# Where the norm sums of a two-block model stand, and in which order its stages open

## What is computed

```python
# first stack, 2 layers
h = rmsnorm(x, norm_g); proj = h @ w_in          # 7592 columns
log_cum = cumsum(log_sigmoid(a_f + b_f))         # a_f: 8 "forget" columns
y_a, y_b, y_c = three attentions of 8 heads (the first one with log_cum)
merged = sum_n sigmoid(gate_n) * ((y_n * silu(z_n)) @ w_branch[n])
x = x + merged @ w_out
x = rmsnorm(x, final_g)                          # between the stacks
# second stack, 2 layers
h = rmsnorm(x, mix_norm_g); u = h @ w_in_2
retention (with rotary q, k), state space, gated linear attention, mLSTM
x = x + merged @ w_out_2
h = rmsnorm(x, ffn_norm_g)
layer 0: x = x + (silu(h @ w1) * (h @ w3)) @ w2  # 2816 hidden
layer 1: x = x + top-2 of 8 experts of that form
x = rmsnorm(x, final_norm_g)
```

## Time and profile before

| | us |
|---|---|
| three timed runs | 2573.23, 2573.83 (median), 2574.51 |
| the profiled execution | 2568.81 |
| its span | 2567.0 |
| PE busy with matmuls | 2390.4 |
| DVE busy | 1699.7 |
| ACT busy | 1263.9 |
| granted clock, mean share of full | 0.965 |

### The profile page before, as it was taken

How to read it: one execution, slowest core, us unless ns; L and a number is a source line. 1 busy time by engine, 2 the same in 40 slices (tenths; PEclk the granted TensorE clock), 3 DMA queues, 4 the chain that set the end, 5 groups by cost and what they waited for, 6 DMA issues and landing times.

```text
span 2567.0 us, 38254 instructions
## 1 busy us (share of the span) xinstructions
PE 2390.4 (93%) x15110; PEld 2016.9 (79%) x15110; DVE 1699.7 (66%) x2630; ACT 1263.9 (49%) x1793; POOL 18.1 (1%) x35
## 2 busy tenths in 40 slices
PE   8999989999999989779998989789999999999997
PEld 7878888878788978679997878677777777777775
DVE  4455674456676557663325557658889889898896
ACT  4435534535543333342214343337767667677664
POOL 0000000000000000000000000000000000000000
PEclk9999999999999989889998989889999999999999
DMA  5433333433373433254443433219989999898893
GB/s 174 128 115 99 99 115 124 136 115 116 102 173 116 149 99 99 99 181 136 160 141 114 145 110 101 99 36 412 353 331 354 344 341 349 339 352 345 332 352 136
DMA packets 255352, 489.12 MB, mean 191 GB/s; under 512 B 35096, under 2 KB 208696, under 8 KB 221128
## 3 DMA queue, kind: packets, MB, share of 16 engines
q1 hardware_dynamic: 249648, 483.87, 53.5%
q10 hardware_dynamic: 4872, 1.09, 0.2%
q0 software_dynamic: 656, 1.71, 0.2%
HBM read 485.57 MB, written 1.05 MB: 190 GB/s over the span
## 4 chain that ended last, share of the span: by engine, by line
PE 70%; DVE 10%; ACT 3%; issue 2%; DMA 1%; DVEq 0%; SPq 0%; ACTq 0%
PE bank L1024 24%; PE bank L689 19%; PE bank L714 9%; PE bank L559 5%; DVE memr L1838 3%; PE bank L541 3%; PE bank L977 2%; PE bank L728 1%; PE bank L497 1%; PE bank L664 1%; PE bank L1065 1%; DVE mem_high L2313 1%; DVE mem_high L2271 1%; PE bank L474 1%; ACT memr L1453 1%
## 5 line engine op out<-in xcount | busy, mean ns | idle before, releaser
L1024 PE MATMUL bank<-memr 128*128 128x256 f32 (+5 forms) x8016 | 1060.5, 293 | 78.4 <-DVE memr L1838 29.3
L1024 PEld LDWEIGHTS bank<-memr 128*128 128x128 f32 (+3 forms) x8016 | 1006.2, 191 | 124.9 <-DVE memr L1838 34.4
L883 DVE TENSOR_TENSOR memr_tail<-mem_tail,memr_ring 128x2048 fp32r<-128x2048 f32 x198 | 451.9, 2288 | 60.8 <-ACT memr_ring L780 58.6
L689 PE MATMUL bank<-memr_ring,memr 128*104 128x512 f32 x1492 | 467.3, 399 | 3.2 <-DVE memr L888 3.2
L1838 DVE TENSOR_TENSOR memr<-mem_low,memr 128x1024 fp32r<-128x1024 f32 (+2 forms) x316 | 378.9, 1215 | 131.3 <-ACT memr L1453 131.0
L780 ACT CAST memr_ring<-mem_tail 128x2048 fp32r<-128x2048 f32 x198 | 379.4, 1916 | 130.9 <-PE bank L689 88.9
L1453 ACT CAST memr<-mem_low 128x1024 fp32r<-128x1024 f32 (+2 forms) x316 | 324.5, 1042 | 186.0 <-PE bank L1024 173.4
L689 PEld LDWEIGHTS bank<-memr_ring,memr 128*104 128x104 f32 x1492 | 250.7, 168 | 95.2 <-issue 3.3
L714 PE MATMUL bank<-memr_ring,memr 128*104 128x512 f32 x752 | 242.4, 400 | 1.7 <-DVE memr_ring L883 1.7
L689 PE MATMUL bank<-memr_tail,memr 128*104 128x512 f32 x536 | 211.4, 394 | 0.0
L714 PEld LDWEIGHTS bank<-memr_ring,memr 128*104 128x104 f32 x752 | 125.3, 168 | 43.3 <-DVE memr_ring L883 1.9
(11 more groups left out here) (247 smaller groups left out, 2221.6 us busy)
## 6 DMA issues: line engine op xcount, KB each, us to landing
mem_tail<-in_moe SPq DMA_DIRECT2D x198, 1024.0 KB, 4.9
mem_low<-in_w_in SPq DMA_DIRECT2D x112, 1024.0 KB, 5.0
mem_high<-in_moe SPq DMA_DIRECT2D x33, 1024.0 KB, 4.8
mem_low<-in_moe SPq DMA_DIRECT2D x33, 1024.0 KB, 4.9
mem_high<-in_ffn_w SPq DMA_DIRECT2D x30, 1024.0 KB, 8.3
mem_low<-in_w_branch SPq DMA_DIRECT2D x20, 1024.0 KB, 4.9
mem_low<-in_w_out SPq DMA_DIRECT2D x16, 1024.0 KB, 5.2
mem_low<-in_w_in SPq DMA_DIRECT2D x6, 512.0 KB, 3.8
```

Source lines behind the costliest of these rows:

```text
L689: ins = pe.matmul(ACC[g % 2][0:CAP, :], h_[e % 2][:, kk, :], w_[:, 512 * k:512 * k + 512], start=(kk == 0 and i == 0), stop=(kk == KT - 1 ...
L883: TTn(raw_r[n % RAW], raw[n % RAW], hi_f[n % HI], ALU.subtract).then_inc(family("m_split"), 1)
L1024: ins = pe.matmul(out(bank), lhsT, rhs, start=((k, i) == order[0]), stop=((k, i) == order[-1]))
```

## The change

1. **Norm sums.** `square_sum` adds the square of tile j-1 right after unit j of `wo` or `wo2`; the last one stands behind the last unit. The sum is built in bank `XB` (between the stacks a second one in `OB`) and `root_of_sum` reads it there. The first norm of all uses the same form without anything between; the norm ahead of the second mixing layer and the last norm stay as they were.
2. **Opening.** `gemm3_two` issues the first two units of a stage side by side: all products with `hh` of unit 0, then of unit 1, then those with `hl` of unit 0 and of unit 1. It is used for `fq` (both layers) and `rq` (both layers). Feed-forward tile 0 gets the same order for its halves. DVE now scales all tiles first and makes the low parts after.
3. **Forget columns.** `ff` and `z 0` come right after `fq`; the chain on DVE and ACT is cut in pieces that lie between the `fk` units.
4. **First feed-forward tile.** Its high parts are cast after the squares 6 and 7 of the residual (ACT), its low parts made ahead of the norm (DVE), and each half has a semaphore of its own.
5. **Rotary.** The matmul for `rk 1` stands after unit `gz 0`.

```diff
+            def gemm3_two(names, ch, cols, m, lo, n, key):
...
+                two = [open_group(name) for name in names]
+                kinds = ((high, hh, "h_high"), (low, hh, None), (high, hl, "h_ready"))
+                for part in ((0, 1), (2,)):
+                    for name, bank, c0 in zip(names, two, cols):
+                        for k in range(KT):
+                            for i in part:
+                                w_, h_, event = kinds[i]
+                                if event and name is names[0]:
+                                    pe.wait_ge(*at(event, key, k))
+                                ins = pe.matmul(bank[0:m, lo:n], w_[:, k, c0:c0 + m], h_[:, k, lo:n], ...
+            def square_sum(bank, key, k, n, lo=0, weights=None):
+                pe.wait_ge(*at("squares", key, k))
+                ins = pe.matmul(bank[:, lo:n], weights(k) if weights else const("ones"), sq[:, k, lo:n], ...
+            def mix_sum(k):
+                square_sum(XB, ("mix", 0), k, T, 0, lambda k: pc("final_w", k).broadcast_to((P, P)))
+                square_sum(OB, ("mix", 0), k, T)
...
+                    if nm == "fq":
+                        ch = split_chunk(win, l, 1536, 1672)
+                        feat3(("ff", l), ch, 0, 8, TA)
+                        feat3(("z", l, 0), ch, 8, P, TA, lo=m0)
...
+                    if l == DEPTH - 1:
+                        if j == 0:
+                            pe.wait_ge(*at("final_w"))
+                        else:
+                            mix_sum(j - 1)
+                    elif j:
+                        square_sum(XB, l + 1, j - 1, TA)
...
+                gemm3_two((("rq", l, 0), ("rq", l, 1)), ch, (0, P), P, 0, T, ("mix", l))
...
                     feat3(("gz", l, j), ch, j % 2 * P, P, T)
+                    if j == 0:
+                        rope2(("rk", l, 1))
...
                     feat3(("wo2", l, j), ch, j % 2 * P, P, T, key=None if j else ("merged2", l))
+                    if j:
+                        square_sum(XB, ("ffn", l), j - 1, T)
+                square_sum(XB, ("ffn", l), KT - 1, T)
... ACT
+                def first_up(k):
+                    if k >= KT - 2:
+                        up_high(0, k - (KT - 2))
... DVE, in both norms
-                    if then and k:
-                        then(k - 1)
                 if then:
-                    then(KT - 1)
+                    for k in range(KT):
+                        then(k)
... DVE, after the last wo2
+                    if l == 0 and j == KT - 1:
+                        low_up(0, 0)
+                        low_up(0, 1)
```

More of the change, by code:

```diff
@@ L1510, in _ @@
                         ahead(nm, l, j)
+                        if nm == "fk" and j == 1:
+                            st.settle()
+                            st(A(asc[0:8, 2, :], asc[0:8, 1, :], ACT.Ln, bias=1.0), sig("logf_ln", l))
+                    if nm == "fq":
+                        act.wait_ge(*evacuated("ff", l))
+                        st(A(asc[0:8, 0, :], tsc[0:8, 3, :], ACT.Abs))
+                        z_tile(0)
+                        st.settle()
+                        st(A(asc[0:8, 1, :], asc[0:8, 0, :], ACT.Exp, scale=-1.0))
                 for c in range(2):
@@ L1515, in _ @@
                     ahead("fv", l, 2, c)
-                act.wait_ge(*evacuated("ff", l))
-                st(A(asc[0:8, 0, :], tsc[0:8, 0, :], ACT.Abs))
-                st.settle()
-                st(A(asc[0:8, 1, :], asc[0:8, 0, :], ACT.Exp, scale=-1.0))
-                st.settle()
-                st(A(asc[0:8, 2, :], asc[0:8, 1, :], ACT.Ln, bias=1.0), sig("logf_ln", l))
-                def z_tile(j):
-                    b = full(act, "z", l, j)
-                    st(A(zs[:, j, m0:], b[:, m0:TA], ACT.Tanh, scale=0.5), sig("z_tanh", l, j))
-                    ahead("z", l, j)
-                for j in range(4):
+                for j in range(1, 4):
                     z_tile(j)
@@ L1799, in _, with normalise @@
             st(V.tensor_scalar(fw, fw, EPS, None, ALU.add), sig("final_w"))
-            def normalise(name, slot, gcol, src, dst, tiles, done, n=TA, d0=0, lo=0, then=None):
-                dve.wait_ge(*evacuated(*name))
+            def normalise(root, slot, gcol, src, dst, tiles, done, n=TA, d0=0, lo=0, then=None):
+                dve.wait_ge(*root)
                 st.settle()
@@ L1810, in normalise @@
                        done(i) if done else None)
-                    if then and i:
-                        then(i - 1)
                 if then:
-                    then(KT - 1)
+                    for k in tiles:
+                        then(k)
             def low_tile(key, k, src, slot, n, lo=0):
```

192 lines of the change are left out of this document (115 added, 77 removed).

## The result

| | before | after |
|---|---|---|
| median of four timed runs, us | 2573.53 | 2546.86 |
| the profiled execution | 2568.81 | 2546.35 |
| its span | 2567.0 | 2544.5 |
| PE busy | 2390.4 | 2378.4 |
| span less PE busy | 176.6 | 166.1 |

What follows compares the result with a forecast made beforehand. PE was taken as the bound, busy 2390.4 of 2567.0 us. Terms 14.2 - 2.9 - 5.6 - 2.4 + 2.7 + 1.0 + 1.8 + 2.2 gave 11.0 us won, so 2573.83 became 2562.8; range 2554 to 2571.5.

Steps and rivals of the forecast that it cites:

- The openings: First two units of a stage: 3.0 us won over three, less 0.3, plus 1.0 between the stacks.
- Rival (c): Openings: the clock stays up as PE gets work twice as fast, 13.6 us more won, 2549.2; chance 0.06.
- The first feed-forward tile: Feed-forward tile 0: from last product to tile 0's end 20.5 us instead of 22.3, so 1.8 won.
- 4 or 5: Sign of a right forecast: the feed-forward wait goes down from 10.98 us to 4 or 5.
- The price of a lone matmul: Norm sums between products: each moves the next unit by 0.72 us, where one in a row costs 0.45.
- rival (a): Norm sums: one between two products costs only 0.45 us, so 6.7 more is won, 2556.1; chance 0.08.
- the sign of part 1: Norm sums between products: roots come later, not earlier, by 2.4 to 5.6 us at each seam; a loss.
- The forget columns: Behind ff in both layers: stops of 4.91 and 5.07 us and their low clock vanish, 14.2 won.
- Rival (d): Forget columns: the chain stops PE in its new place too, the 14.2 us is gone, 2577.0; chance 0.06.
- Rotary: Matmul of rk 1 moved behind gz 0: 1.1 us won, twice, so 2.2.
- the only case below 2554: Rival (c), the clock up in the openings, at 2549.2 us; chance 0.06.

Runs made afterwards that it cites:

- a_again: The changed kernel run again with nothing altered, as a yardstick: median 2546.19 us, 0.9904 of the time before.
- o_open: Kernel before, with only part 2 (openings side by side, DVE scaling first) added: 2557.11 us, 0.9950 of the time before.
- o_first: Kernel before, with only part 4 (first feed-forward tile split ahead of the norm) added: 2563.97 us, 0.9976 of the time before.
- u_first: Changed kernel without part 4, the first feed-forward tile split behind the norm again: 2547.45 us, 0.9914 of the time before.
- o_sums: Kernel before, with only part 1 (norm sums between the residual products) added: 2579.77 us, 1.0037 of the time before.
- u_sums: Changed kernel without part 1, all norm sums in a row behind the last product: 2532.44 us, 0.9856 of the time before.
- u_rope: Changed kernel without part 5, both rotary matmuls of rk ahead of gz 0 again: 2543.43 us, 0.9904 of the time before.

## Why the prediction was wrong

**The openings are the step that failed.** The forecast put the gain of an opening at 1.0 us: eight products by 2.9 us after the first scaling, then "6.8 us at 0.23 each" of low clock, then the rest, 11.0 in all. It took what the clock does, and where it does it, as fixed. Ahead of layer 1 the opening took 8.8 us, not 11.0. The low stretch has its old length, but it begins 1.7 us ahead of the first scaling, not 2.9 behind it: of its 6.8 us only 4.04 fall on busy PE, the rest on the reciprocal, the first scaling and the cast, for which PE waits. In the first norm and ahead of the second mixing layer the stretch shrank from 6.8 to 3.4. From the first scaling to the second unit's evacuation the four openings took 11.7, 12.1, 11.3 and 11.9 us and take 9.4, 8.8, 8.9 and 9.5: 10.4 gained, where 3.7 was forecast. In a_again, the same program, they take 10.0, 9.8, 10.1 and 9.7: 7.4 gained, although three of them hold a stretch of 6.8 us. Its opening ahead of layer 1, with the window over the low stretch:

```profile
401.46 3.39 DVE L1889 SCALAR_TENSOR_TENSOR mem_low<-mem_high 128x272 f32<-128x272 f32 x8
411.22 0.37 ACT L1583 COPY mem_high<-bank 64x256 f32<-64x256 f32 x1 [0.17 <-PE bank L1053]
...
401.80:408.60 6.80, 6.04 (x28) 6.07 (x29) 6.80 (x17) 3.31 (x8) 0.00 (x0) 0.50 0.00 0
```

So the price of a product at the low clock was right (28 products in the stretch, where 29 were forecast). What was wrong is that eight would be done ahead of it: it begins with the scalings, and the other 20 run behind it at full speed. The working priced DVE's order and PE's together; alone DVE's brings 12.7, PE's nothing. Rival (c), the clock up in the openings, named the right place, but its condition, 1.00 all through, is not what happened, and openings and first tile together brought 9.3 more than forecast between the profiles, not its 13.6. In o_open, 13.2 us faster, the time that PE stands still is unchanged (177.1 against 176.6), and busy PE is 13.9 shorter; half of what it is less in low stretches (120.2 us instead of 145.7) is 12.8. So nearly all of it is the clock. Why a denser supply in the opening leaves fewer low stretches elsewhere, these runs do not show.

**The first feed-forward tile** was another term off, by the same 11.0: 1.8 forecast. The wait fell by 6.6 to 4.40, as the "4 or 5" named for a right step, and the low stretch there from 10.2 to 3.4. The delays by ACT's cast and DVE's subtraction are as worked out: the root starts 1.98 after the last product (forecast 2.15 to 2.6), the reciprocal, at 1115.06 behind the subtraction, 3.43 (forecast 3.4), and it is done at 5.2, as forecast. From the first scaling to tile 0's end, where the forecast had 11.0, it took 8.7 (9.2 in a_again). From the root to tile 0's end it is 18.7 before and 11.9 after; 12.0 in o_first, and 17.5 in u_first. So the part is worth 5.6 to 6.7 us at its place, alone and in the changed kernel. The timed runs gave 6.4 alone and 1.3 undone: PE's standing still moves by 7.4 and 5.1, but the part raises PE busy, by 2.6 in o_first and by 4.0 between u_first and the changed kernel, and in the second that eats the gain.

**The price of a lone matmul** failed too, and moved the sum by 4.7 us. Forecast 0.72, as "this very situation". It was not: in the earlier trace rows the neighbour waited for a bank, and a sum in `XB` takes no bank from anybody. Periods of the units, by the times at which DVE takes them up: 2.83 us before and 3.26 with a sum between, 3.02 and 3.47 with 272 columns, 3.67 with two sums. So a sum costs 0.43, 0.45 and 0.42. The Trainium skill, "TensorE: Matmul & The Clock Gate", section "Step-by-step: what each phase is for", has the weights of the next matmul loaded during the present one; the trace agrees (0.43 between two products, 0.45 in a row), and the prediction should have asked why a row spoke against it. Its premise for rival (a) held.

Rival (a), a chance of 0.08, wanted 6.7 more from this (6 x 0.27 x 4 is 6.5). 4.7 came at the four seams; the rest went into the first sum of each, whose square is late. So the sign of part 1 stays as forecast. DVE's rows of the last and of the second unit ahead of the experts are 20.03 us apart, before 16.96: 3.07 more, since the first sum, whose square is late, adds 0.9, and five add 0.43. The root comes 1.73 after the last one, before 3.46. Net +1.3; ahead of the feed-forward +1.4, ahead of layer 1 +1.6, between the stacks 5.55 more and 1.24 less, +4.3. Together 8.6, where 13.3 was forecast, and o_sums measured 8.9. So PE is full there: six of the eight sums push the last product out by as much as they take from behind it, and the chain of last evacuation, square and sum, 1.7 us that ran beneath the other sums, now stands alone. In the changed kernel the part costs 13.8; of the 15.0 between the spans 6.7 is standing still, the rest the clock (8.9, see u_sums). Why it falls so is not shown.

**The forget columns** went as worked out: both stops are gone with the low clock behind them. From the second unit of the opening to the root of the low-rank norm behind `z` the two traces draw apart by 7.5 us in layer 0 and 6.6 in layer 1: 14.1 against 14.2, and the same 14.1 in a_again. Alone 18.0, undone 11.5: PE's standing still moves by 9.3 and 10.5, near the 9.98 of the earlier trace rows, PE busy by 6.9 and 2.3. Rival (d), a new stop behind `ff`, did not occur.

**Rotary**: forecast +2.2; at its place the part gained 0.7 and 1.0, 1.7 in all, and 4.5 in a_again, where no low stretch falls on the two places. The timed runs can't show it. Before, PE stands for 2.08 and 1.36 there (3.4 us, the second is the earlier trace rows); now `gz 0` waits 2.08 and `gz 1` 0.67. A low stretch of 3.4 us lies on the place before and after (`gz 0` takes 4.61 us). Rows of the changed kernel at that place:

```profile
785.86 4.61 PE L1028 MATMUL bank<-memr 128*128 128x256 f32 x24 [2.08 <-DVE memr L1918]
...
791.56 8.62 PE L1028 MATMUL bank<-memr 128*128 128x256 f32 x71 [0.67 <-DVE mem_high L2147]
```

The prediction saw that a matmul between leaves one bank, and priced it at 0.45 in this one place, while the same effect stood unseen in the earlier trace rows.

**The sum of it.** By the forecast's own terms, measured (forecast) in us: forget 14.1 (14.2), sums -8.6 (-13.3), openings 10.4 (3.7), tile 6.8 from the root to tile 0's end, without its share of the sums (4.2), rotary 1.7 (2.2). Together 24.4, where 22.5 lies between the profiles; the 1.9 too much is within what two traces of one program differ by. Against the 11.0 of the forecast, 6.7 is the openings', 4.7 the sums', 2.6 the tile's, -0.5 the rotary's. The first and third come from laying the old stretch of low clock behind the first products of each opening, the second from taking the wait for a bank for the price of a matmul. The chances gave 0.06 to the only case below 2554.

**What stays open.** What sets the low stretches. They last 3.4, 6.8 or 10.2 us nearly everywhere, but the same program shows them at different places, and a part that is undone changes them in distant stages (u_rope: 8.0 us less of busy PE for moving one matmul in each of two layers). That it is the stretches, and not the products, is shown: take from PE busy half of what of it lies at 0.50, and all 14 traces with the rotaries in `ACC` give 2315.7 to 2319.4, while PE busy itself goes from 2370.1 to 2394.8. For the parts alone standing still adds up (+4.8, +0.5, -9.3 and -7.4, in sum -11.4, measured -10.5), and so does PE busy (+4.4, -13.9, -6.9, +2.6: -13.8, measured -12.0). For the parts undone neither does: standing still comes to +6.7 - 3.1 - 10.5 - 5.1 - 3.1 = -15.1, PE busy to +8.3 - 9.1 - 2.3 + 4.0 + 8.0 = +8.9 (each the changed kernel less the run without the part), where -10.5 and -12.0 were to be explained. Each of these differences holds the same one trace of the changed kernel; with a_again's in its place the two sums are -4.1 and +2.9. So part of the mismatch is chance, and for the rest of PE busy no run here tells the reason.

## What to carry to other kernels

Before a gap on the critical engine is taken as the price of an instruction, look for what else ended with it: here two thirds of the 0.72 us behind a small matmul was a wait for an accumulation bank, and giving those matmuls banks of their own brought 22.1 us, nearly as much as the whole change. Work moved into a stretch in which the engine is full costs its full time there, however cheap it is; it must have been on the path in its old place by more than that. When two kinds of small operation alternate on an engine that feeds the critical one, doing all of the first kind first is worth trying before the critical engine's own order (12.7 us against none). And before a part is credited with what a run without it costs, look at its own place in several traces: part 5 there gained in all of them, while the time of the one run without it moved the other way.

## What the runs showed of the hardware

- A matmul in plain fp32 between products in fp32r costs what it costs in a row: 0.43 us with 256 columns (0.45 in a row), 0.45 with 272 (3.83 / 8 = 0.48 in a row).
- The profile can put a wait for a bank under no releaser at all. The 788.88 of the earlier trace rows bears no bracket, while the same wait in the changed kernel does (idle 0.52, ended by ACT L1706, at 771.02). A short gap without a name is not proof of a fixed cost.
- DVE's eight subtractions of 272 columns take 2.90 us when they stand together, 0.36 each, where a single one takes 0.43; eight scalings take 3.39, 0.42 each, where one takes 0.49 to 0.50. In turn a pair takes 0.77, about as much as when grouped (0.79): what the order changes is not DVE's total but when PE's first eight pairs of products are fed, every 0.42 instead of every 0.77.
- Of the 22.5 us gained between the profiles, 12.0 came with PE's instructions unchanged and without any less standing still; 11.1 of them is half of the 22.1 us that busy PE spent less at 0.50. A change of PE busy between two traces of the same products should be read together with the granted clock before it is credited to the edit.
